# One decoder layer with product-key experts on one core: tile 0 alone ahead of the expert slots, the other tiles between them

## The reference

```
mod = silu(c) @ w_ada + b_ada            # shift1, scale1, gate1, shift2, scale2, gate2
h = rmsnorm(x) * (1 + scale1) + shift1
z = h @ w_in                             # 6656 columns: q, k, v, conv_in (u), gate_post, gate_pre, gate_attn, gate_conv
A = windowed attention (128), 16 heads over 4 key heads, normed q and k, sinks
B = gate_post * conv3(gate_pre * u)
x = x + gate1 * ((sigmoid(gate_attn) * A + sigmoid(gate_conv) * B) @ w_out)
h2 = rmsnorm(x) * (1 + scale2) + shift2
# 8 heads: scores against 2 x 128 keys, the best 16 of 256 pairs, softmax gates
x = x + gate2 * sum over 8 heads x 16 picks of gate * gelu(U[idx] . h2) * V[idx]
```

## Time and profile before

| what | before |
|---|---|
| median of 3 runs | 3891.65 us (3890.81 to 3892.19) |
| the profiled execution | 3892.44 us |
| its span | 3890.4 us |
| PE, DVE, ACT, POOL busy | 3279.5, 2530.7, 1077.4, 2407.8 us |
| granted TensorE clock | 0.967 of full |
| HBM read and written | 1238.54 and 20.55 MB |

### The profile page before, as it was taken

The page is one execution under the profiler, slowest core; times in us unless marked ns, Lnnn a source line. Parts: engine busy times, 40 slices in busy tenths (PEclk is TensorE's granted clock), DMA queues, the critical chain, the costliest instruction groups (busy, mean ns, idle before and its releaser), DMA issues.

```text
span 3890.4 us, 35676 instructions
## 1 busy us (share of the span) xinstructions
PE 3279.5 (84%) x10638; PEld 1724.2 (44%) x10638; DVE 2530.7 (65%) x5905; ACT 1077.4 (28%) x2400; POOL 2407.8 (62%) x2146
## 2 busy tenths in 40 slices
PE   4899995997999999999978778867887788789777
PEld 1457773444555655566534233423342334334221
DVE  2355546666887776787746677667766876776663
ACT  1225551222322322243212223213221323222220
POOL 1000003777667777766757777777777777776775
PEclk7999998999999999999989999999999999999999
DMA  6452225999999999999999999999999999999998
GB/s 217 160 172 71 60 60 186 345 373 382 367 356 371 385 384 351 390 353 348 357 392 363 370 358 351 363 358 365 372 365 360 372 369 376 368 374 336 370 364 316
DMA packets 466874, 1259.47 MB, mean 324 GB/s; under 512 B 42071, under 2 KB 171415, under 8 KB 466014
## 3 DMA queue, kind: packets, MB, share of 16 engines
q0 software_dynamic: 304128, 1107.43, 76.0%
q1 hardware_dynamic: 141290, 136.46, 10.7%
q10 hardware_dynamic: 21268, 13.32, 1.1%
HBM read 1238.54 MB, written 20.55 MB: 324 GB/s over the span
## 4 chain that ended last, share of the span: by engine, by line
PE 32%; DMA 25%; POOL 20%; DVE 9%; issue 9%; ACT 5%; SPq 0%; DVEq 0%; ACTq 0%; POOLq 0%
PE bank L1746 19%; DMA v_ring<-in_expert_v_dram,idx 18%; POOL u_ring L674 10%; POOL v_ring L682 10%; PE bank L1574 6%; DMA u_ring<-in_expert_u_dram,idx 5%; DVE u_ring L1349 2%; PE bank L1715 2%; PE bank L1770 1%; PE bank L1696 1%; DMA mod_s<-mod 1%; PE bank L1553 1%; ACT sm L768 1%; DVE rt L1132 1%; ACT sm L777 1%
## 5 line engine op out<-in xcount | busy, mean ns | idle before, releaser
L1746 PE MATMUL bank<-v_ring,diag 128*128 128x512 f32 (+1 forms) x4224 | 2068.8, 620 | 487.4 <-DMA v_ring<-in_expert_v_dram,idx 389.5
L1349 DVE CUSTOM_DVE_ANT_0 u_ring<-u_ring,h2b 128x1024 f32<-128x1024 f32 x1056 | 1286.8, 1225 | 877.7 <-DMA u_ring<-in_expert_u_dram,idx 835.9
L674 POOL DMA_INDIRECT u_ring<-in_expert_u_dram,idx x1056 | 1186.2, 1123 | 767.9 <-DVEq L1330 393.3
L682 POOL DMA_INDIRECT v_ring<-in_expert_v_dram,idx x1056 | 1206.4, 1142 | 475.1 <-PE bank L1746 239.9
L1746 PEld LDWEIGHTS bank<-v_ring,diag 128*128 128x128 f32 (+1 forms) x4224 | 754.0, 192 | 1555.6 <-DMA v_ring<-in_expert_v_dram,idx 830.5
L920 ACT ACTIVATE diag<-ident,wgt 128x128 f32<-128x128 f32 x1024 | 357.3, 394 | 664.2 <-PE bank L1746 310.1
L1574 PE MATMUL bank<-hi,whi 128*128 128x512 f32 x832 | 413.1, 497 | 2.4 <-issue 2.4
L1574 PE MATMUL bank<-hi,wlo 128*128 128x512 f32 x832 | 328.9, 395 | 0.0
L1574 PE MATMUL bank<-lo,whi 128*128 128x512 f32 x832 | 327.6, 394 | 0.0
L1126 DVE TENSOR_TENSOR wlo<-wc,whi 128x1024 fp32r<-128x1024 f32 x104 | 127.4, 1226 | 123.2 <-ACT whi L733 117.6
L1574 PEld LDWEIGHTS bank<-hi,whi 128*128 128x128 f32 x832 | 159.0, 191 | 75.5 <-issue 51.2
(11 more groups left out here) (259 smaller groups left out, 2607.4 us busy)
## 6 DMA issues: line engine op xcount, KB each, us to landing
wc<-in_w_in_dram SPq DMA_DIRECT2D x104, 512.0 KB, 5.9
ada_w<-in_w_ada_dram SPq DMA_DIRECT2D x12, 2048.0 KB, 8.1
u_ring<-in_expert_u_dram,idx POOLq DMA_INDIRECT x1056, 6.4
v_ring<-in_expert_v_dram,idx POOLq DMA_INDIRECT x1056, 6.4
wo_sb<-in_w_out_dram SPq DMA_DIRECT2D x2, 4096.0 KB, 19.1
wq_sb<-in_w_query_dram SPq DMA_DIRECT2D x2, 4096.0 KB, 28.1
xt<-in_x_prompt_dram SPq DMA_DIRECT2D x8, 512.0 KB, 4.9
out_dram<-h2b SPq DMA_DIRECT2D x8, 512.0 KB, 6.9
```

The costliest lines, as they stand in the source:

```text
L674: pool.indirect_dma_start(out=u_ring[k % RING][:, :], out_offset=None, in_=eu, in_offset=bass.IndirectOffsetOnAxis(ap=idx[n % IDXS][:, k:k ...
L682: pool.indirect_dma_start(out=v_ring[k % RING][:, :], out_offset=None, in_=ev, in_offset=bass.IndirectOffsetOnAxis(ap=idx[n % IDXS][:, k:k ...
L1349: V.tensor_tensor_reduce(out=u_ring[k % RING][:, :], in0=u_ring[k % RING][:, :], in1=h2b[t % 2][:, :], scale=1.0, scalar=0.0, op0=ALU.mult ...
L1746: last = M(banks(c, 1)[0:parts, :], diag[k % DIAGS][:, 0:parts], v_ring[k % RING][:, c * 512:(c + 1) * 512], start=first, stop=final)
```

## The change

- Ahead of the slots only tile 0 is prepared. Its 128 tokens are now the stationary side and w_in the moving one, in 13 columns of 512, each loaded, cast and split in two units of 1 MB (ring of three). Its q and k are normed along the free axis and transposed (`transpose_job`); eight attention pairs.
- The shift and scale of the first norm are made directly as columns (`modulation_columns`: weights stationary, 9 columns moving, four blocks of w_ada) and applied on ACT behind the transpose; the other eight blocks go as before, beside the first eight columns.
- Tiles 1 to 4 are one group, tiles 5 to 7 with the samples another (416 tokens, the samples among the moving columns). Each group has its own pass over w_in of 52 blocks: group 0 from slot 0, one block every 1.35 slots, a whole block in one slot; group 1 from slot 280, one every 5.45, in four pieces. v comes first. The ring of w_in's tiles and of their high and low parts is three deep each (four and two before).
- All tiles but 0 are parked and reloaded. Attention of tiles 1 to 7 starts at slots 24, 84, 142, 190, 500, 642, 770, a pair every 4 or 5 slots. w_out and w_query are loaded three times.
- In units 0 to 3, picks k with k % 4 in (1, 2) are added by DVE into `y_sum`, with no diagonal and no matmul; the sum is added in PSUM at slot 82.

```diff
-HT = NT // 2
-WRING = 4
-P2_FIRST = 112
-P2_PITCH = 6.0
-D_BASE = (0, 32, 64)
-PARKED = (2, 3)
+GROUPS = ((1, 2, 3, 4), (5, 6, 7))
+WRING = 3
+UNIT_RING = 3
+PBANKS = (2, 3, 7)
+PARKED = (3, 4)
+P_FIRST = (0, 280)
+P_PITCH = (1.35, 5.45)
+NORM_AT, NORM_STEP = 266, 3
+WO_AT = (71, 571)
+ATTN = (None, 24, 84, 142, 190, 500, 642, 770)
+A_PITCH = (None, 4, 5, 4, 4, 5, 5, 5)
+D_BASE = (None, 78, 142, 187, 233, 579, 690, 818, 930)
+SPLIT_HI, SPLIT_LO = (-3, -6), (-2, -4)
+PIECES = ((0,), (0, 1, 3, 4))
+DVE_UNITS = 4
+FOLD_AT = 82
+def on_dve(n, k):
+    return n < DVE_UNITS and k % 4 in (1, 2)
...
+            def column_matmuls(i):
+                for u in (2 * i, 2 * i + 1):
+                    w(u_split, u + 1)
+                    r = u % UNIT_RING
+                    for k in range(HALF):
+                        at = u % 2 * HALF + k
+                        for x, wt in ((hi0, uhi), (lo0, uhi), (hi0, ulo)):
+                            last = M(banks(i % 2, 1), x[:, at, :], wt[r][:, k, :], ...)
...
+            def load_w(at):
+                if at >= WRING:
+                    sp.wait_ge(w_split, at - WRING + 1)
+                sp.dma_start(wc2[at % WRING][:, :, :], w_cols(at % NPROJ)).then_inc(wc_in[at % WRING], 16)
...
+            def load_attn(t):
                 for r in range(2):
+                    sp.wait_ge(qkv_parked[r], 16 * (QKV // P // 2) * (group_of(t) + 1))
+                sp.wait_ge(merged, t)
...
+            sp.wait_ge(u_split, NUNIT)
+            sp.wait_ge(pT_ps, KC)
+            sp.dma_start(wo_first[:, :, :], w_out_v).then_inc(wo_in, 16)
+            sp.wait_ge(unit_ps, NUNIT)
+            sp.dma_start(wq_first[:, :, :], w_query_v).then_inc(wq_in, 16)
...
             def gather_v(n, k):
                 if at >= RING:
-                    pool.wait_ge(rows_done, at - RING + 1)
+                    if on_dve((at - RING) // TOPK, (at - RING) % TOPK):
+                        pool.wait_ge(rows_added, dve_rows(at - RING))
+                    else:
+                        pool.wait_ge(rows_done, pe_rows(at - RING))
...
+            def add_row(n, k):
+                w(v_in[k % RING], 16 * (at // RING + 1))
...
+                    ins = V.scalar_tensor_tensor(out=y_sum[:, :], in0=v_ring[k % RING][:, :],
+                                                 scalar=wgt[n % 2][:, k:k + 1], in1=y_sum[:, :], op0=ALU.mult, op1=ALU.add)
```

More of the change, by code:

```diff
@@ L80, in d_base, with group_of, pe_rows, dve_rows @@
[L80 to L89, removed]
+def group_of(t):
+    return 0 if t in GROUPS[0] else 1
+DVE_UNITS = 4
+FOLD_AT = 82
+def on_dve(n, k):
+    return n < DVE_UNITS and k % 4 in (1, 2)
+def pe_rows(at):
+    return sum(not on_dve(i // TOPK, i % TOPK) for i in range(at + 1))
+def dve_rows(at):
+    return at + 1 - pe_rows(at)
@@ L192, in build @@
[L192 to L213, removed]
@@ L231, in build @@
         sink_col = place("sink_col", 46680, NKV)
-        sm1 = row([f"sm1_{r}" for r in range(SM_RING)], 31872, 2, 2 * P)
-        pT1 = row(["pT1_0", "pT1_1"], 16384, 2, 2, P)
         sm2 = place("sm2", 47616, 2, 2 * P)
@@ L452, in _ @@
[L452 to L471 removed]
+            sp.wait_ge(cols_ps, 1)
@@ new lines, in keep_hT, with split_unit @@
+                if t < NT:
+                    for k in range(KC):
+                        link.note(nc.scalar.activation(out[:, k, :], ps[:, k, :], ACT.Identity, scale=A1c[:, k, NB:NB + 1],
+                                                       bias=mod_c[:, k, NB:NB + 1]))
+                    link.settle()
+                    act.sem_inc(tr_read, 1)
+                else:
+                    w(tr_read, job("x8") + 1)
+                nc.scalar.copy(hi, out).then_inc(hi_made, 1)
+            def split_unit(u):
+                w(wu_in[u % UNIT_RING], 16 * (u // UNIT_RING + 1))
+                if u >= UNIT_RING:
+                    w(unit_ps, u - UNIT_RING + 1)
+                nc.scalar.copy(uhi[u % UNIT_RING][:, :, :], wu[u % UNIT_RING][:, :, :]).then_inc(uhi_made, 1)
@@ L1264, in residual, with taps @@
+            def taps(y, cu, c):
+                link(V.tensor_scalar(y, cu(0), cw[:, 0, c:c + 1], cw[:, 3, c:c + 1], ALU.mult, ALU.add))
+                for tap in (1, 2):
+                    link(V.scalar_tensor_tensor(out=y, in0=cu(tap), scalar=cw[:, tap, c:c + 1], in1=y, op0=ALU.mult, op1=ALU.add))
             def residual(j, parts):
@@ L1738, in add_row @@
             def add_row(n, k):
+                if (n + 1) * TOPK + k == FOLD_AT:
+                    w(rows_added, DVE_UNITS * TOPK // 2)
+                    for c in range(2):
+                        last = M(banks(c, 1), ident[:, :], y_sum[:, c * 512:(c + 1) * 512], start=False, stop=False)
+                    last.then_inc(rows_folded, 1)
+                if on_dve(n, k):
+                    return
                 at, parts = n * TOPK + k, P if n < NT * PH else NS
```

1502 lines of the change are left out of this document (811 added, 691 removed).

## The result

The changed kernel takes **3934.85 us** (median of 7 runs), the kernel before 3892.19 us beside it: ratio 1.0087, 95% interval [1.0056, 1.0118]. It is 0.9% slower (the ratio is taken over undisturbed executions, the medians over all). The forecast was 3800 us, in a range of 3700 to 3890, with 0.85 on faster. Its profiled execution took 3919.6 us, with a span of 3917.6.

The account below looks back on a forecast made before the run. PE bounds the front before the first expert gather, DMA bytes the expert stage after it. First gather 297 + 4.5 to the first dot + 400 for slots 0 to 70 + 3100 = 3801.5, said as 3800 us; range 3700 to 3890.

Parts of the forecast that it names:

- The frame: Whole kernel: time to the first gather, 4.5 us to the first dot, slots 0 to 70, then the rest.
- Modulation columns: Front, before column 0: 256 narrow instructions at 0.11 us, 28 us, plus 6 for a cold start.
- Eight columns with a modulation block: Front: TensorE paces eight columns at 12.3 us, 98, plus 15 for jobs, three pairs and a slow clock.
- front bound by ACT and DVE: Rival, front: eight columns at 15 us and five at 20 instead of 12.3 and 15; +47, total 3847; chance 0.17.
- Five columns: Front's last columns, with five attention pairs: 75 us between PE's 48 and ACT's serial 100; last transposes and merge 6.
- Slots 0 to 70: First expert slots with four tiles' projection: PE's 367 us of work over 0.92 gives 400; bounds 367 and 460.
- The rival of late w_in tiles: Slots 0 to 70: late w_in tiles make the kernel slower, from 490 us in this stretch on; chance 0.13.
- The rest: From slot 70 to the end: bytes decide, 3053 + 33 + 20 - 6 = 3100 us; bounds 3060 and 3140.
- New w_out 7 slots after its issue: After slot 70: the reloaded w_out is needed some 20 us after issue but lands in 24.3, so 5 us stall.
- Attention at pitch 4: After slot 70: in-order waits from three more tiles of attention, 3 x 6 and some for tighter pitch, 20 us.
- Bytes: After slot 70: net 13.6 MB more to move, 37 us at 367 GB/s, taken as 33.
- The rule weighed: ACT table switches: the sum used 1.28 us each; the skill's some 2.66 would make the total about 3824.

Follow-up runs that it names:

- With rows: First four modulation blocks made as rows with the weights moving in 512 columns, then transposed, against the changed kernel; ratio 1.0012 to the kernel before.
- the run of five edits: Changed kernel with modulation rows, bias ahead of the split, gates first, wider attention pitch, and POOL's queue with later cache copies; 3822.69 us, ratio 0.9791.
- The last run's two edits: Onto the five edits: three modulation rows read behind the last w_in tile, and late columns' pairs ahead of later tiles' pieces; 3816.11 us, ratio 0.9798.

## Why the prediction was wrong

**The frame held.** Front set by hand-overs and TensorE, then 70 slots set by TensorE, then bytes. The forecast's sign failed because three terms of the front and two of the rest were too small, so that of a forecast lead of 136 us at slot 70 (334 - 198) 57 were there, and the 84 us that the rest costs more than before (3136.5 - 3053, forecast 47) used it up.

**Front, 297 forecast, 401.9 measured. This is the step that failed: above all the eight columns, "8 x 12.3 = 98" with 15 for the rest, which took 163 because of the order on in-order queues; then the five late columns and the modulation columns.**
- *PE ready, norm and transposes, 23 us*: they began at 22.5 and ended at 24.3.
- *Modulation columns, 256 x 0.11 + 6 = 34 us*: 54.6. "Twice that while the clock is at its lower level" stood beside it, and six were taken for it; the pace is that of the lower level to the end. Column 0 began at 85.3 instead of 62. With rows it began at 61.3 to 62.2.
- *Eight columns with a modulation block, 113 us*: 163 (85.3 to 248.4), 20.4 each with jobs and first pairs (the expectations' 18.9 is a plain one). The 12.3 were TensorE's work, right to 0.3 us in columns 1 and 2 once the ring was cut. What the forecast left out is the order on VectorE: its bullet names what each engine has to do, not in which order, and for the rival "front bound by ACT and DVE" it said that in the first eight "nothing but casts and lo parts stands against 12.3". The bias stood there, and TensorE waited for it. Moving it gave 27 of the 50. Of the rest, some 23, the later edits gave some 4, and 19 are left, in columns 3 to 7. They are not the landing of w_in's tiles, for which no cast waited in the run of five edits; the chain shows the same kind of order on VectorE with `aq` in it, and in column 7 the first pairs. That is read from a trace and not tested. ScalarE was busy 46 and VectorE 66 of 164 us here (84 to 248), so the rival had the direction, but the work of those two engines was not the reason.
- *Five columns, 75 us, and 6 for the merge*: 109 (248.4 to 357.8), past the upper bound of 100 + 6 by 3. ScalarE was busy 64 of them and TensorE 59, so neither is a bound; each pair is handed round in turn, and every cast, norm and transpose in the queues lies in that round. The last run's two edits gave 12 of the 28.
- *w_out to first gather, 41.5*: 44.0.
- After all edits the first gather comes at 334.3, just inside the forecast's bounds of 265 to 340; 19 us of what remains is in the first eight columns and 17 in the last five.

**Slots 0 to 70, 400 forecast, 372 measured.** The sum of 367 for TensorE was right (357 busy); the factor of 0.92, set near another stretch's 0.94, was too cautious: 367 are 0.99 of the 372. VectorE's sum of 322 came out as 308. The V rows on VectorE, forecast at 49 us, are worth 36.5. The rival of late w_in tiles is not seen: the largest waits in this stretch end with TensorE or VectorE, and no wait there ends with a w_in tile (the largest of the changed kernel, 402 to 781 us: total, times, longest).

```profile
POOL v_ring L745 <- PE bank L1934: 88.4, 23, 5.4
POOL u_ring L732 <- DVE dot L1506: 69.3, 23, 8.9
ACT whi L921 <- PE bank L1958: 55.6, 12, 6.4
POOL v_ring L745 <- DVE y_sum L1520: 34.4, 16, 4.5
```

**The rest, 3100 forecast, 3136.5 measured.** Its sum has a slip of 2 us: 5 of stall and 9 credited make -4, and -6 was added. Two terms were too small:
- *New w_out 7 slots after its issue, "5 of stall"*: slots 70 to 80 took 71 us, 41 more than before. The forecast had the 5 here, and of its 33 for bytes the 29 of w_out, w_query and the rows (10.5 MB at 367 GB/s). The reload itself landed in 23.8 us, as forecast. What was missed is who else was in the queue: the last y store behind it and ayg behind that, on which the merge and w_out wait. The order alone gave 14 us back at this place; what is left is 12 MB beside the gathers, with DMA at 0.94 then.
- *Attention at pitch 4, "20"*: it was costed as 6 us a tile "and some for the tighter pitch". Pitch 5, with the merges later, gave 30 us back by slot 240.
- *Bytes*: the forecast's 33 us for 13.6 MB more. The windows give 1129 MB from slot 70 on in the changed kernel and 1112 in the one before (sums of length by GB/s), 17 more. In the stretch of the second group's projection (slots 288 to 560) the forecast had no gain; there the changed kernel runs at 380 GB/s and made 23 us good, most of which it gave back at its own reload behind slot 560. With pitch and order mended, 3136.5 - 30 - 14 = 3092, and the last version took 3095 from slot 70 to its end (713.7 to 3809.0), next to the 3100.

**The rule weighed** (the Trainium skill, "ScalarE: Activation LUTs", What ACT_TABLE_LOAD costs) came out as the row of before had it. In the changed kernel's front a load and what follows it (start, us):

```profile
250.51 1.28 ACT L833 ACT_TABLE_LOAD   x1 [0.17 <-ACT esink L847]
251.81 0.60 ACT L833 ACTIVATE ug<-bank 128x512 f32<-128x512 f32 x1
```

1.28 us and the next activation 0.02 behind; no drain as long as the page's follows it. What the late columns took too long is not that.

**The chances.** The range ended at 3890, its upper bounds together gave 3947, and these were called unlikely together. Of the five upward misses one is the clock's (the modulation columns). The other four have one root as far as the runs show: sums of work were taken where order on in-order queues decides. Such terms do not err independently. That the total stayed below 3947 is luck: the front ended 62 us past its own upper bound of 340, and slots 0 to 70 ended 88 below theirs.

## What to carry to other kernels

When a stage is split into rings across engines, write down for each engine the order of its instructions and follow one buffer round: a small step queued behind a large one (here 0.7 us of bias behind a split) cost TensorE some 3 us a turn, 27 us in all, until it was moved. A store that somebody waits for goes out ahead of bulk loads, and the load that the next stage needs first goes first, over both queues, SP's and ScalarE's. That gave 14 us where the next stage waited for a small transfer, and nothing at the second such place, where DMA was at its full rate anyway. A front shortened by spreading its work over a stage that is DMA-bound wins only as long as that work keeps the gathers going, and a hand-over chain that is started again before it is over holds them up: of the two pitches tried here the looser was faster.

## What the runs showed of the hardware

- TensorE's clock fell while it made narrow matmuls without a break: 9 moving columns with 128x128 weights ran at 0.116 us at a granted clock of 0.96 at first, and then at 0.213 us at 0.50 to their end 46 us later. In the changed kernel 256 of them took 54.6 us at the pace of the lower level; the same products with 512 columns moving took 29. The Trainium skill ("TensorE: Matmul & The Clock Gate", Part 1: The HAM clock gate) says that "activity releases the throttle"; here the clock stood at the lower level, and fell to it, while the engine was busy without a break, so this trace does not bear the sentence out for such matmuls.
- A store of 256 KB took 2.5 us to land, and 24.8 us when 8.4 MB of loads had been issued from the other queue 1 us before it.
- The PEclk column read 1.00 for the first 90 us of a trace in which the pace of the matmuls was the lower level's: ahead of the first record of the clock it says nothing.
